# Up-projection in pairs of blocks, with one row group of a pair in seven block products instead of eight

## What is computed

```python
def sq_relu_mlp(h, w_up, w_down):
    return jnp.square(jax.nn.relu(h @ w_up)) @ w_down

for l in range(DEPTH):                       # DEPTH = 2
    ...                                      # attention
    x = x + sq_relu_mlp(rms_norm(x, mlp_norm_g[l]), w_up[l], w_down[l])
return rms_norm(x, final_norm_g)
```

## Time and profile before

| | us |
|---|---|
| median of 3 executions | 2004.65 (2004.22 to 2005.13) |
| the profiled execution, its own time | 2004.46 |
| its span in the trace | 2002.6 |
| TensorE busy | 1993.8 |
| VectorE (DVE) busy | 1501.3 |
| ScalarE (ACT) busy | 1022.8 |
| GpSimd (POOL) busy | 28.2 |

### The profile page before, as it was taken

One profiled execution on the slowest core, in us unless ns is written; L12 is line 12 of the kernel. 1 busy time (PEld: TensorE's weight loads), 2 busy tenths in 40 slices (PEclk: granted clock), 3 DMA queues, 4 the chain that ended last, 5 costly groups with the idle time before them and its releaser, 6 DMA issues.

```text
span 2002.6 us, 26143 instructions
## 1 busy us (share of the span) xinstructions
PE 1993.8 (100%) x9212; PEld 1665.9 (83%) x9212; DVE 1501.3 (75%) x1897; ACT 1022.8 (51%) x1319; POOL 28.2 (1%) x29
## 2 busy tenths in 40 slices
PE   9999999999999999999999999999999999999998
PEld 7888888888888888888888998888888888888887
DVE  7789998866856776785698787976776785686665
ACT  6555555444544544454556665544444454454443
POOL 0000000000000000000010000000000000000010
PEclk9999999999999999999999999999999999999999
DMA  8655545666566567656665554566566656656663
GB/s 308 209 172 188 182 165 173 208 211 220 200 200 223 186 209 225 215 199 205 206 207 174 140 150 148 193 227 206 193 221 205 222 201 197 222 194 203 221 226 110
DMA packets 252854, 398.82 MB, mean 199 GB/s; under 512 B 17648, under 2 KB 75376, under 8 KB 252784
## 3 DMA queue, kind: packets, MB, share of 16 engines
q1 hardware_dynamic: 217104, 379.03, 56.8%
q10 hardware_dynamic: 35680, 18.88, 3.5%
HBM read 379.00 MB, written 2.10 MB: 190 GB/s over the span
## 4 chain that ended last, share of the span: by engine, by line
PE 97%; DMA 1%; ACT 0%; DVE 0%; issue 0%; SPq 0%; ACTq 0%; POOLq 0%; POOL 0%; DVEq 0%
PE acc L541 27%; PE acc L539 27%; PE acc L540 27%; PE acc L559 2%; PE acc L560 2%; PE acc L561 2%; PE side L788 1%; PE side L789 1%; PE side L787 1%; PE acc L787 1%; PE acc L789 1%; PE acc L788 1%; PE acc L863 1%; PE acc L864 1%; PE acc L865 1%; DMA raw<-in_a_w_qkv 0%
## 5 line engine op out<-in xcount | busy, mean ns | idle before, releaser
L1542 DVE TENSOR_TENSOR wlo<-raw,whi 128x1024 fp32r<-128x1024 f32 (+1 forms) x652 | 778.4, 1214 | 258.6 <-ACT whi L1010 256.4
L1010 ACT ACTIVATE whi<-raw 128x1024 fp32r<-128x1024 f32 (+1 forms) x652 | 670.0, 1047 | 535.7 <-PE acc L541 381.6
L539 PE MATMUL acc<-whi,opA 128*128 128x512 f32 (+2 forms) x1296 | 501.8, 387 | 0.0
L541 PE MATMUL acc<-whi,opA 128*128 128x512 f32 (+2 forms) x1296 | 500.9, 387 | 0.0
L540 PE MATMUL acc<-wlo,opA 128*128 128x512 f32 (+2 forms) x1296 | 500.9, 386 | 0.0
L539 PE MATMUL acc<-whi,opB 128*128 128x512 f32 x1104 | 431.0, 390 | 0.1
L541 PE MATMUL acc<-whi,opB 128*128 128x512 f32 x1104 | 429.8, 389 | 0.0
L540 PE MATMUL acc<-wlo,opB 128*128 128x512 f32 x1104 | 429.5, 389 | 0.0
L539 PEld LDWEIGHTS acc<-whi,opA 128*128 128x128 f32 x1296 | 243.4, 188 | 48.9 <-issue 0.4
L540 PEld LDWEIGHTS acc<-wlo,opA 128*128 128x128 f32 x1296 | 243.4, 188 | 48.7
L541 PEld LDWEIGHTS acc<-whi,opA 128*128 128x128 f32 x1296 | 243.4, 188 | 48.5
(11 more groups left out here) (333 smaller groups left out, 1748.5 us busy)
## 6 DMA issues: line engine op xcount, KB each, us to landing
raw<-in_w_up SPq DMA_DIRECT2D x128, 1024.0 KB, 5.6
raw<-in_w_down SPq DMA_DIRECT2D x128, 1024.0 KB, 5.1
raw<-in_a_w_qkv SPq DMA_DIRECT2D x44, 1024.0 KB, 5.1
raw<-in_a_w_o SPq DMA_DIRECT2D x16, 1024.0 KB, 5.0
prob<-junk ACTq DMA_DIRECT2D x128, 128.0 KB, 5.6
raw<-in_b_w_o SPq DMA_DIRECT2D x16, 1024.0 KB, 5.0
raw<-in_w_ukv SPq DMA_DIRECT2D x32, 256.0 KB, 4.2
raw<-in_w_dkv SPq DMA_DIRECT2D x4, 1024.0 KB, 5.0
```

The lines of the kernel that those rows point to most:

```text
L539: mm(o, a_hi, w_hi, start=start, stop=False)
L541: done = mm(o, a_lo, w_hi, start=False, stop=last and c == chunks - 1)
L1010: done = fn(whi[:, place:place + ch, 0:n], raw[:, r, c0:c0 + ch, 0:n], ACT.Copy)
L1542: done = tt_(wlo[:, place:place + ch, 0:n], raw[:, r, c0:c0 + ch, 0:n], whi[:, place:place + ch, 0:n].bitcast(F32), ALU.subtract)
```

## The change

Seven of the eight pairs of up blocks (all but the first pair of each MLP's first quarter) are now computed in pairs: three row groups in the ordinary way, and the first row group (chunks 0 to 3 of `opA`) in seven products. Order on TensorE (`up_pair`): six halves of block b in `acc[1]`, the seven products, six halves of block b+1 in `acc[0]`. The sums of activations for it (`x_forms`) are made once per MLP. The side banks are no longer zeroed once and gathered over all quarters: behind every pair, up or down, ACT copies the four banks and DVE combines them (`combine`, four instructions of 128x512). For an up pair the result of a block is then `acc` plus a combined share, which DVE adds into `up_sq` (`sum_first`, `sum_second`), and relu and square become two ACT instructions (`square_sums`). The DVE squaring and the GpSimd work go away. `move_quads`, `hid_high`, `hid_low` and `up_turn` stand in new places. The core of the diff, on TensorE:

```diff
+                def up_pair(q, i):
+
+                    b = B_MLP[l] + 2 * JB * q + 2 * i
+                    uses = [u[k] + U_QUARTER * q + i for k in range(2)]
+                    for hf in range(6):
+                        half_tok(b, hf, 1, chunks_of(opA, 4 + 2 * hf), first=hf == 0, uses=uses[1])
+                    shares_free(up_shares(l, q, i))
+                    pe.wait_ge(form_lo, FORM_SETS * l + 1)
+                    seven(up_groups(l, q, i), i - 1, b, 6, opA, 0, x_forms, uses[0], True, True)
+                    for hf in range(6):
+                        half_tok(b + 1, hf + 2, 0, chunks_of(opA, 4 + 2 * hf), first=hf == 0, last=hf == 5, uses=uses[0],
+                                 starts=(False, True))
```

On ScalarE:

```diff
-                def drain_up(q, j):
-
-                    used(B_MLP[l] + 2 * JB * q + j)
-                    fn(up_sq, acc[(j + 1) % 2][:], ACT.Copy).then_inc(drained[(j + 1) % 2], 2)
...
+                def square_sums(q, i, k):
+
+                    s, n = 1 - k, 2 * up_pairs(l, q, i) + k + 1
+                    act.wait_ge(drained[s], 2 * (u[s] + U_QUARTER * q + i) + 2)
+                    fn(up_sq, up_sq, ACT.Relu).then_inc(relu_done, 1)
+                    act.wait_ge(relu_done, n)
+                    fn(up_sq, up_sq, ACT.Square).then_inc(sq_done, 1)
...
+                def up_pair(q, i, after):
+
+                    b = B_MLP[l] + 2 * JB * q + 2 * i
+                    def down_copy(k):
+                        fn(down_shared[k], side[k], ACT.Copy).then_inc(shared_copied, 1)
+
+                    split(b, 3)
+                    if after == "up":
+                        square_sums(q, i - 1, 1)
+                    elif after == "down":
+                        down_copy(0)
+                    split(b, 4)
+                    if after == "up":
+                        hid_high(q, 2 * i - 2)
+                    elif after == "down":
+                        down_copy(1)
+                    split(b, 5)
+                    if after == "down":
+                        down_copy(2)
+                    else:
+                        move_quads(q, 2 * i - 1)
+                    between = {"B22": lambda: down_copy(3)} if after == "down" else {
+                        "B21": lambda: hid_high(q, 2 * i - 1)}
+                    seven(up_groups(l, q, i), i - 1, b, 6, (3, b), (0, b + 1), between)
+                    for hf in range(2, 6):
+                        split(b + 1, hf)
+                    act.wait_ge(pe_halves, 8 * b + 10)
+                    if after == "down":
+                        act.wait_ge(shared_added, 2 * ((QUARTERS - 1) * l + q))
+                    for k in range(4):
+                        fn(up_shared[k], side[k], ACT.Copy).then_inc(shared_copied, 1)
+                    split(b + 1, 6)
+                    split(b + 1, 7)
+                    square_sums(q, i, 0)
+                    split(b + 2, 0)
+                    split(b + 2, 1)
+                    move_quads(q, 2 * i)
+                    split(b + 2, 2)
...
+                def last_chain(q):
+
+                    return {3: lambda: square_sums(q, 1, 1), 4: lambda: hid_high(q, JB - 2),
+                            5: lambda: move_quads(q, JB - 1), 7: lambda: hid_high(q, JB - 1)}
```

On VectorE:

```diff
-                def square_up(q, j):
-
-                    s = (j + 1) % 2
-                    dve.wait_ge(drained[s], 2 * (u[s] + U_QUARTER * q + j // 2 + 1))
-                    stt(out=up_sq, in0=up_sq, scalar=0.0, in1=up_sq, op0=ALU.max, op1=ALU.mult).then_inc(sq_done, 1)
...
+                def sum_second(q, i):
+
+                    used(B_MLP[l] + 2 * JB * q + 2 * i + 1)
+                    dve.wait_ge(shared_sums, 4 * up_shares(l, q, i) + 4)
+                    dve.wait_ge(sqT_done, JB * (QUARTERS * l + q) + 2 * i + 1)
+                    for t in range(TT):
+                        tt_(up_sq[:, t, :], acc[0][:, t, :], up_shared[2 * t + 1], ALU.add).then_inc(drained[0], 1)
...
+                def up_pair(q, i, follows):
+
+                    b = B_MLP[l] + 2 * JB * q + 2 * i
+                    if follows == "up":
+                        sum_second(q, i - 1)
+                    split(b, 3)
+
+                    def after_first():
+                        if follows != "down":
+                            up_turn(q, 2 * i - 1)
+                        split(b, 4)
+                        if follows == "up":
+                            hid_low(q, 2 * i - 2)
+
+                    after = {"first sum": after_first, "second sum": lambda: split(b, 5)}
+                    if follows == "down":
+                        after["third sum"] = lambda: down_combine(q - 1)
+                    else:
+                        after["B11"] = lambda: hid_low(q, 2 * i - 1)
+                    seven(up_groups(l, q, i), i - 1, b, 6, (3, b), (0, b + 1), 8 * b + 3, after)
+                    split(b + 1, 2)
+                    if follows == "down":
+                        down_add(q - 1)
+                    for hf in range(3, 6):
+                        split(b + 1, hf)
+                    combine(up_shares(l, q, i), up_shared)
+                    split(b + 1, 6)
+                    sum_first(q, i)
+                    split(b + 1, 7)
+                    up_turn(q, 2 * i)
+                    for hf in range(3):
+                        split(b + 2, hf)
+
+                def last_chain(q):
+
+                    return {3: lambda: up_turn(q, JB - 1), 4: lambda: hid_low(q, JB - 2), 7: lambda: hid_low(q, JB - 1)}
```

More of the change, by code:

```diff
@@ L416, in pair, with up_pair @@
                         quad(b + i // 4, i % 4, src, later=int(i == 6))
-                with sp.Fori(0, JB) as j:
+                by_quarter = W_UP[l].rearrange("p c (q n) -> p c q n", q=QUARTERS)
+                def up_pair(q, i, quarters, at, after_pair=False):
+                    b = B_MLP[l] + 2 * JB * q + 2 * i
+                    order = ((0, 1), (0, 2), (0, 3), (0, 0), (1, 0), (1, 1), (1, 2), (1, 3))
+                    for k, (j, r) in enumerate(order):
+                        col = NB * (2 * i + j)
+                        src = quarters[:, 4 * r:4 * r + 4, bass.ds(at, 1), col:col + NB].rearrange("p c a n -> p c (a n)")
+                        quad(b + k // 4, k % 4, src, later=int(k == 7 or after_pair and k == 1))
+                with sp.Fori(0, 2) as j:
                     up(0, j)
+                up_pair(0, 1, by_quarter, 0)
                 with sp.Fori(0, QUARTERS - 1) as q:
@@ L1300, in seven, with down_forms @@
+                def down_forms(q, g, nth):
+                    form_high(forms[g][:, 0], FORM_SETS * l + 2 * q + nth + 1)
+                def seven(group, at, b, hf0, own, other, between):
+                    (o, o_loads), (t, t_loads) = own, other
+                    source = {"B11": raw[:, o, 0:2, :], "B21": raw[:, o, 2:4, :], "B22": raw[:, t, 2:4, :],
+                              "T1": w_sum, "T2": raw[:, t, 2:4, :], "T3": raw[:, t, 0:2, :], "T4": w_sum}
                     for f in FORMS:
@@ L1310, in seven @@
+                            place = extra_place(l, at, f)
+                            fn(extra_hi[:, place:place + 2, :], source[f], ACT.Copy).then_inc(extra_hi_ready, 1)
                         else:
@@ L2062, in seven @@
                     tt_(b22, w_sum, b22, ALU.add).then_inc(w_summed, 1)
-                    low("B21", g, q, b, hf0, b21)
+                    if "third sum" in after:
+                        after["third sum"]()
+                    low("B21", group, at, b, hf0, b21)
                     dve.wait_ge(w_summed, n + 3)
@@ L2098, in mlp @@
+                up_pair(0, 1, "plain")
                 with dve.Fori(0, QUARTERS - 1) as q:
+                    sum_second(q, 1)
                     for j in range(2):
@@ L2107, in mlp @@
                     pair(q)
-                    up(q + 1)
+                    up_pair(q + 1, 0, "down")
+                    up_pair(q + 1, 1, "up")
+                sum_second(QUARTERS - 1, 1)
                 q = QUARTERS - 1
```

293 lines of the change are left out of this document (158 added, 135 removed).

## The result

The changed kernel takes 2044.49 us (median, 2041.68 to 2048.07), against 2004.77 us for the kernel before beside it: a ratio of 1.0199, 95% interval 1.0186 to 1.0212. It is 2.0% slower. The profiled execution took 2048.07 us, the slowest of the four, with a span of 2046.3 us.

The account below looks back on a forecast made before the run. TensorE bounds the kernel, busy 1993.8 of 2002.6 us, with 1.0 us to spare in the chain to half 6. 2004.46 - 16.0 + 29.6 + 11.4 = 2029.5, rounded down to 2028 us; range 2011 to 2048.

Parts of the forecast that it names:

- 84 matmuls for 16.0 us: TensorE, 14 pairs: 48 matmuls become 42 in seven products, 1.14 us gained each, 16.0 us in all.
- The chain in the first down block: Sum, square, transpose, transfers, `hid_high`, `hid_low`: ends at 19.95 us, half 6 due at 16.32; TensorE stands for 3.6 us.
- 8.04 us: Time from the transfers' first issue to `hid_high`, mean of 32 groups in the kernel before, used for the moved issue.
- The term of 29.6 us: Loss before half 6 in eight first down blocks, 3.7 us each including some 0.1 for the first matmul.
- The step down from 2029.5 to 2028: Sum rounded down, as transfers issued while TensorE stands were said to meet fewer loads.
- transfers return in time: Rival: first issue to `hid_high` takes 4.4 us or less, no stalls, only the gain stays: 1988.5 us; chance 0.05.
- The estimate of some 4.3 us: Transfer time behind the fourth issue by the Trainium skill, about 2.0 us plus bytes; set aside for the trace.
- The waits in the products: Six up pairs behind up pairs: fourth product 0.8 us late, fifth 0.9, with restarts 1.9 each, 11.4 us in all.
- `hid_low` ahead of T2: In those up pairs DVE does `hid_low` before lo of the fifth product: 23.6 against 22.7 us, 0.9 us lost.
- The clock: Rival: behind the stalls halves 6 and 7 run at 1.2 GHz, 4.8 us a block, 38 in all: 2067 us; chance 0.08.
- a clock below full: Sign that the forecast is wrong: the clock in the changed kernel's profile page drops below full.
- the upper bound: Transfers at 9.51 us make the stalls 5.2 and 3.4 us: 2050 us; as rival of slow transfers, chance 0.07.

Follow-up runs that it names:

- Experiment 2: The changed kernel with a second buffer for the moved pieces, so transfers no longer wait for the previous block's `hid_low`: 1989.21 us, ratio 0.9921.
- experiment 7: The changed kernel with one 1 MB weight load held back until lo of half 7 instead of half 5: 2005.83 us, ratio 1.0006.
- experiment 5: The two-buffer kernel of Experiment 2 with four short ACT copies ahead of the last up block's transfers, issuing them later: 2037.66 us, ratio 1.0159.
- experiment 4: The changed kernel with the previous block's `hid_high` and `hid_low` moved behind the last product, in up pairs behind up pairs: 2039.41 us, ratio 1.0176.
- Experiment 1: The changed kernel with 16 unread matmuls ahead of half 6 of each quarter's first down block: 2031.21 us, ratio 1.0128.
- experiment 3: The kernel before with four unused DVE additions ahead of the transpose of each quarter's last up block: 2041.19 us, ratio 1.0178.
- experiment 6: The changed kernel with `sum_second` ahead of lo of half 2 on DVE, behind up pairs, one buffer: 2025.45 us, ratio 1.0107.
- experiment 8: The changed kernel with the edits of experiment 6 and experiment 7 together, still one buffer: 2000.35 us, ratio 0.9977.

## Why the prediction was right, and where it wasn't

Slower, as forecast (2028 us, measured 2044.49, inside the range of 2011 to 2048). By its own steps:

**84 matmuls for 16.0 us: right.** Experiment 2, where nothing waits, is 15.6 us below the kernel before.

**The chain in the first down block: right nearly to the digit.** `sum_second` at 1.6 (measured 1.54), issue at 9.5 (9.46), 8.04 us to `hid_high` (8.20 here, mean 8.17), end at 19.95 (20.04). The term of 29.6 us measured 30.2, without the first matmuls that it had counted in. The step down from 2029.5 to 2028, for fewer loads beside the transfers, had nothing behind it: 8.17 us is more than 8.04.

**Its unstated assumption: wrong in kind, and right by luck.** The 8.04 us, a mean of 32 groups of before, were taken as a property of the transfers, with a range of 7.58 to 9.51. They depend on when one weight load is issued: 4.7 us when it is held away (experiment 7) or the transfers are 3.5 us ahead of it (experiment 2), 8.1 when two buffers are there but the issue is late (experiment 5). The rival "transfers return in time" named this, "later issues fall into another phase of the weight loads", and got 0.05 because no group of before came under 7.58. That row could not speak for it: in the trace of the kernel before, SyncE issues a load 1.2 to 1.3 us behind the first transfer of every one of the 32 groups, so their number says nothing of another phase. Here the phase stayed the same (1.2 to 1.4 us in the eight blocks), so the number held. The estimate of some 4.3 us rests on a figure that the Trainium skill (DMA: Bandwidth & Descriptors, Anatomy of one DMA) gives for transfers issued by GpSimd; these are issued by ACT, so by that section it is no price for them. The trace comes near it only with no load beside the transfers: the fourth lands 4.60 to 4.81 us behind the first issue in experiment 7.

**The waits in the products: 11.4 forecast, 9.2 in gaps and some 1.4 in restarts measured; the place right, half of the cause wrong.** The step that failed is "there at 18.0. ACT: `hid_high` to 19.0, only then hi of the fourth product". The transfers were there early (`hid_high` 5.7 us behind the issue, with no wait, in the pair of experiment 4's rows) and B11 was late because its row on DVE stood behind the four issues. The other half, `hid_low` ahead of T2, was right (experiment 4).

**The clock: the failed step.** It was written as a rival for itself, 4.8 us a block and a chance of 0.08, so that the forecast held a stall of 3.7 us with a clock at full. The profiled execution has both: seven of eight stalls were followed by 8 to 14 slow matmuls, 17.6 us in all, a mean of 2.5 for each of the seven; not 24 matmuls and 4.8 us. The clock was back at full by about the end of half 6. Experiment 1 shows the cause, at 13.3 us of the median. The prediction held that no row of the kernel before shows such a fall. One does: TensorE's last matmul starts at 1995.01, and from 1998.00 on the granted clock is at 0.50:

```profile
1998.00:2002.00 4.00, 0.00 (x0) 0.00 (x0) 0.69 (x2) 0.13 (x1) 0.00 (x0) 0.50 0.70 262
```

The Trainium skill (TensorE: Matmul & The Clock Gate, What's actually happening) says that an idle array is put back to the lower clock; by that rule the clock term belonged to the forecast's own stalls. The granted clock of 0.50 behind seven of the eight agrees; behind the eighth it did not fall. With 2029.5 + 13.3 - 0.8 (up pairs) + 0.6 the sum would be 2043, against 2044.5. The prediction had named a clock below full as a sign that it is wrong, and by the span's mean of 0.988 that sign came. The time lies inside the range all the same, which is luck: the upper bound was made of slow transfers, with nothing for the clock, and the slow matmuls cost less than half of what the rival had put at them.

The change failed by a chain of three: DVE's sums and `hid_low` made the issue late; a load issued 1.3 us behind it, as in the kernel before, kept the transfers at 8 us; and the stall lowered the clock. The same edit with a second buffer gains 0.8%.

## What to carry to other kernels

A transfer's duration read from a trace holds for its place among the other transfers. Before it is used for a moved issue, look what the queues carry at the new time, and what releases that. Where a chain cannot be made shorter, moving one large load that has time to spare may be worth more than any reordering: here 39 us for one wait of the load queue. What ties the two together deserves a look first: with one buffer, transfers and load followed the same `hid_low`, and starting the chain earlier moved both. And when a wait of several microseconds appears on TensorE, add the slow matmuls behind it to its price, not to a rival's.

## What the runs showed of the hardware

- Four transfers of 128 KB on ACT's queue, 0.67 us from issue to issue: the fourth lands 7.8 to 8.6 us behind the first issue where a 1 MB load of SyncE is issued 1.2 to 1.4 us behind it (the eight first down blocks of the changed kernel; 7.6 to 9.5 in the 32 groups before). It lands after 4.60 to 4.81 us where the load is issued some 6.4 us behind (experiment 7), and after 4.6 to 4.7 in seven of eight blocks where it is 3.5 behind (experiment 2; once 6.0). The runs show no more of how the load delays them than that the DMA engines are busy meanwhile.
- The clock does not answer to the length of a stall alone. In the changed kernel stalls of 3.8 us were followed by no slow matmul once and by 8 to 13 in the other three; in experiment 3 gaps of 2.8 to 2.9 us by none three times and by 6 to 9 five times. The drop also came up to 1.5 us behind the stall's end (experiment 6). In experiment 4, with stalls of 3.45 to 4.11 us, all eight cost 1.4 to 1.6 us, and in the changed kernel up to 3.0. What picks the one or the other stays open. It goes with a wider scatter: 6.4 us between executions of the changed kernel, 0.3 in experiment 2.
- Above the span of experiment 2, the gaps, slow matmuls and restarts explain all 11.7 us of experiment 8, and 47.5 of the 48.9 us of experiment 4; where the other 1.4 us lie wasn't found.
